# Operand copies on another engine, row sums from the matrix product, and a new order of units in an encoder step

## The reference, cut to what matters

```python
h = rmsnorm(x); u = h @ w_in                  # mixer columns, memory queries, gate
A: softmax(q k^T / 8 + bias) v                # 12 heads of 64, band of 8 chunks of 64 tokens
B: o = (softmax(q1 k1^T/8 - alibi) - lam * softmax(q2 k2^T/8 - alibi)) v   # 6 heads, v of 128
   o = rmsnorm(o)
C: q = rmsnorm(cq) @ w_uq                     # 12 heads of 64 + 32 rotated columns
   k, v = rmsnorm(ckv) @ w_ukv                # latent of 256, values of 64
   softmax((qn kn^T + qr kr^T) * scale) v     # chunk-causal, all earlier keys
M: softmax(mq mk^T / 8) mv
x += (concat(mixer, M) * silu(gate)) @ w_out
```

## Time and profile before

| | |
|---|---|
| median of 3 runs | 3321.17 us (3317.43 to 3321.68) |
| profiled execution: time, span | 3319.59 us, 3317.7 us |
| mean granted clock of PE | 0.91 of full |
| PE busy | 2822.7 us (85%) |
| VectorE busy | 1540.5 us (46%) |
| ScalarE busy | 1216.2 us (37%) |
| GpSimd busy | 834.4 us (25%) |
| chain that ended last | PE 64%, VectorE 17%, ScalarE 10%, issue 4%, GpSimd 4% |

### The profile page before, as it was taken

The page is one execution under the profiler, slowest core; times in us unless marked ns, Lnnn a source line. Parts: engine busy times, 40 slices in busy tenths (PEclk is TensorE's granted clock), DMA queues, the critical chain, the costliest instruction groups (busy, mean ns, idle before and its releaser), DMA issues.

```text
span 3317.7 us, 46359 instructions
## 1 busy us (share of the span) xinstructions
PE 2822.7 (85%) x18786; PEld 2631.0 (79%) x18786; DVE 1540.5 (46%) x3502; ACT 1216.2 (37%) x2680; POOL 834.4 (25%) x434
## 2 busy tenths in 40 slices
PE   4888999978979889879888677777779888999987
PEld 4788999978878878869877566667669788999877
DVE  7205565551135666751222256665651215655542
ACT  3323444432234444442232234434341224444431
POOL 7522222204322122204311222222203312212212
PEclk8999999989989999979997878888879999999989
DMA  3311111113111111113110000000013111111111
GB/s 143 101 49 38 54 51 45 55 63 103 40 39 49 55 58 52 49 62 94 54 39 27 23 13 9 6 9 6 14 49 98 55 39 51 45 47 59 51 66 65
DMA packets 55892, 167.90 MB, mean 51 GB/s; under 512 B 6464, under 2 KB 14272, under 8 KB 55168
## 3 DMA queue, kind: packets, MB, share of 16 engines
q1 hardware_dynamic: 55680, 164.94, 14.7%
HBM read 131.13 MB, written 33.79 MB: 50 GB/s over the span
## 4 chain that ended last, share of the span: by engine, by line
PE 64%; DVE 17%; ACT 10%; issue 4%; POOL 4%; DMA 1%; SPq 0%; DVEq 0%; ACTq 0%
PE acc L1363 30%; PE acc L1342 9%; PE acc L1426 8%; PE scores L1384 8%; PE turned L1396 5%; ACT prob L957 5%; DVE prob L1155 3%; DVE pt_split L1185 3%; PE scores L1295 2%; POOL h_split L1237 2%; DVE raw L1043 2%; ACT pt_split L966 2%; DVE prob L1178 2%; DVE prob L1175 1%; POOL w_lo L1229 1%
## 5 line engine op out<-in xcount | busy, mean ns | idle before, releaser
L1363 PE MATMUL acc<-h_split,w_hi 128*128 128x352 f32 (+3 forms) x5116 | 1263.3, 330 | 84.4 <-POOL w_lo L1229 40.6
L1363 PEld LDWEIGHTS acc<-h_split,w_hi 128*128 128x128 f32 x5116 | 899.6, 194 | 109.0 <-POOL w_lo L1229 44.4
L1229 POOL TENSOR_TENSOR w_lo<-w_raw,w_hi 128x1024 fp32r<-128x1024 f32 (+2 forms) x172 | 390.1, 2271 | 1946.5 <-ACT w_hi L916 1946.5
L1363 PE MATMUL acc<-h_split,w_lo 128*128 128x352 f32 (+3 forms) x2558 | 833.2, 326 | 0.0
L957 ACT ACTIVATE prob<-prob,stat 128x256 f32<-128x256 f32 (+9 forms) x576 | 386.0, 671 | 532.1 <-DVE stat L1155 532.0
L1426 PE MATMUL acc<-pt_split,v_split 128*64 128x256 f32 (+4 forms) x3486 | 487.4, 280 | 73.5 <-DVE pt_split L1185 63.5
L1185 DVE TENSOR_TENSOR pt_split<-turned,pt_split 128x512 fp32r<-128x512 f32 (+4 forms) x564 | 303.0, 552 | 519.3 <-ACT pt_split L966 518.7
L1363 PEld LDWEIGHTS acc<-h_split,w_lo 128*128 128x128 f32 x2558 | 496.2, 194 | 0.0
L1426 PEld LDWEIGHTS acc<-pt_split,v_split 128*64 128x64 f32 (+1 forms) x3486 | 389.2, 156 | 98.5 <-DVE pt_split L1185 81.0
L1396 PE MATMUL turned<-ident,prob 128*128 128x128 f32 (+2 forms) x1866 | 301.4, 287 | 147.4 <-DVE prob L1179 86.2
L1155 DVE CUSTOM_DVE_ANT_0 prob<-scores,bias 128x256 f32<-128x256 f32 (+9 forms) x576 | 338.1, 633 | 186.2 <-PE scores L1384 182.9
(11 more groups left out here) (102 smaller groups left out, 2805.4 us busy)
## 6 DMA issues: line engine op xcount, KB each, us to landing
w_raw<-w SPq DMA_DIRECT2D x148, 512.0 KB, 3.5
x_scr<-y_sb SPq DMA_DIRECT2D x24, 528.0 KB, 5.3
y_sb<-x_scr SPq DMA_DIRECT2D x24, 528.0 KB, 5.7
bias<-rel_in SPq DMA_DIRECT2D x24, 320.0 KB, 4.2
raw<-kcache SPq DMA_DIRECT2D x18, 256.0 KB, 3.8
v_cache<-vcache SPq DMA_DIRECT2D x18, 256.0 KB, 3.7
y_sb<-x_in SPq DMA_DIRECT2D x8, 528.0 KB, 5.9
y_out<-raw SPq DMA_DIRECT2D x8, 528.0 KB, 2.7
```

What stands on the lines that cost most here:

```text
L1229: pool.tensor_tensor(w_lo[:, n % 2, 0:wide], w_raw[:, n % 2, 0:wide], w_hi[:, n % 2, 0:wide].bitcast(F32), ALU.subtract).then_inc(wlo_made ...
L1363: ins = pe.matmul(acc[s.bank][:, 0:s.cols], (w_hi, w_lo)[ws][:, w, 128 * k:128 * k + 128], x(xs, k), start=k == 0 and y == 0, stop=k == s. ...
```

## The change: what it does, and the diff

1. The high halves of queries and keys (`conv`) are copied by ScalarE instead of VectorE. The two parts are cut anew: A, B: first 512 columns; C: half of queries and keys each.
2. In C no probabilities are normalised before the product. Columns of ones stand beside the values' high halves, so that the product with 128 columns gives values in rows 0 to 63 and the sums of the probabilities in rows 64 to 127. ScalarE takes logarithm and exp(-x) of the sums, VectorE multiplies by the gate (`evac`) after the logarithms and by the reciprocals in a new item `emul`. The exponentials write no row sum. The accumulator is free for PE once it was multiplied by the gate.
3. The three passes of pv are in a new order, the outer loop over passes: (value high, p high), (value low, p high), then (value high, p low). PE waits for the chunk's high halves first and for its low halves only before the third pass. All kinds of job.
4. The order of units is 1, 2, 0, 3, 4 for A, B, C, and the side products are spread as (2, 1, 3, 2, 1) for A and B and (3, 3, 5, 3, 1) for C.
5. Buffers: values' halves laid out anew, the probabilities' buffer shorter, some small buffers share places. GpSimd sets the ones once, at the start of layer C.

```diff
+PV_PASSES = ((0, 0), (1, 0), (0, 1))
-PROB = 5632
+PROB = 4928
-    for g in (0, 1, 2, 3) if job.kind == "M" else (0, 2, 1, 3):
+    for g in (0, 1, 2, 3) if job.kind == "M" else (1, 2, 0, 3):
-BESIDE = {"M": (1, 1, 1, 0, 0), "A": (2, 2, 2, 2, 1), "B": (2, 2, 2, 2, 1), "C": (3, 4, 4, 3, 1)}
+BESIDE = {"M": (1, 1, 1, 0, 0), "A": (2, 1, 3, 2, 1), "B": (2, 1, 3, 2, 1), "C": (3, 3, 5, 3, 1)}
                 if narrow:
                     self.scores(nxt, 1)
+                if prev is not None:
+                    order.append(("emul", prev))
-        return (slice(0, 256), slice(0, 256)) if part == 0 else (slice(256, TOK), slice(256, KEYS))
+        return (slice(0, 512), slice(0, 512)) if part == 0 else (slice(512, TOK), slice(512, KEYS))
-            half, quarters = TOK // 2, slice(0, 1) if part == 0 else slice(1, 4)
+            half, quarters = TOK // 2, slice(2 * part, 2 * part + 2)
 ...
 def scalar_program
+                    if u.job.kind != "C":
                         act.activation(p, p, ACT.Exp, scale=-1.0, bias=..., accum_out=...)
+                    else:
+                        act.activation(p, p, ACT.Exp, scale=-1.0, bias=...)
+            elif name == "conv":
+                ... (the waits that VectorE had)
+                for i, (x, hi, _) in enumerate(splits_of(job, part)):
+                    act.activation(hi, x, ACT.Copy).then_inc(operand_hi.mark(job.n, part, i), 1)
+            elif name == "evac" and item[1].job.kind == "C":
+                u = item[1]
+                act.wait_ge(*pv_done.upto(u.chunks[-1].p))
+                if u.before.job.kind == "C":
+                    act.wait_ge(*o_read.upto(u.before.n))
+                for lane in range(2):
+                    act.activation(recip[64 * lane:64 * lane + 64, 0:u.qn], acc[0][64:128, 256 * lane:256 * lane + u.qn],
+                                   ACT.Ln).then_inc(sums_logged.mark(u.n), 1)
+                act.wait_ge(*sums_logged.upto(u.n))
+                act.activation(recip[:, 0:u.qn], recip[:, 0:u.qn], ACT.Exp, scale=-1.0).then_inc(sum_recips.mark(u.n), 1)
 ...
 def vector_program
-            elif name == "conv":
-                ...
-                    dve.tensor_copy(hi, x).then_inc(operand_hi.mark(job.n, part, i), 1)
-            elif name == "N":
+            elif name == "N" and item[1].job.kind != "C":
 ...
+                    if u.job.kind == "C":
+                        dve.wait_ge(*sums_logged.upto(u.n))
                     for lane in range(2):
                         ins = dve.tensor_tensor(gate, acc[0][0:64, ...], gate, ALU.mult)
-                    ins.then_inc(o_read.mark(u.n), 1)
+                    ins.then_inc((o_gated if u.job.kind == "C" else o_read).mark(u.n), 1)
+            elif name == "emul" and item[1].job.kind == "C":
+                dve.wait_ge(*o_gated.upto(u.n))
+                dve.wait_ge(*sum_recips.upto(u.n))
+                dve.tensor_tensor(gate, gate, recip[:, 0:u.qn], ALU.mult).then_inc(o_read.mark(u.n), 1)
 ...
 def pool_program
+                elif what == "operands" and more["kind"] == "C":
+                    pool.wait_ge(*normed_hi.upto(norm_key, KT - 1))
+                    pool.memset(v_hi[:, :, :, 64:128].bitcast(F32), 1.0).then_inc(ones_set.mark("values"), 1)
 ...
 def tensor_program
-                pe.wait_ge(*o_read.upto(held.n))
+                pe.wait_ge(*(o_gated if held.job.kind == "C" else o_read).upto(held.n))
-                if c == 0:
+                if c == 0 and u.job.kind != "C":
                     pe.wait_ge(*probs_ready.upto(u.tiles[-1].n))
+                elif c == 0:
+                    pe.wait_ge(*exps_ready.upto(u.tiles[-1].n, 1))
-                pe.wait_ge(*turned_lo.upto(chunk.a))
+                pe.wait_ge(*turned_hi.upto(chunk.a))
-                for i, (lane, block, n, src, dst, w) in enumerate(chunk.mults):
-                    for y, (vs, ps) in enumerate(PASSES):
+                for y, (vs, ps) in enumerate(PV_PASSES):
+                    if y == 2:
+                        pe.wait_ge(*turned_lo.upto(chunk.a))
+                    for i, (lane, block, n, src, dst, w) in enumerate(chunk.mults):
+                        if job.kind == "B":
+                            rows, values = 128, vb_sp[0:n, vs, block, :]
+                        elif vs == 0 and job.kind == "C":
+                            rows, values = 128, v_hi[0:n, block, lane, :]
+                        elif vs == 0:
+                            rows, values = 64, v_hi[0:n, block, lane, 0:64]
+                        else:
+                            rows, values = 64, v_lo[0:n, block, lane, :]
```

More of the change, by code:

```diff
@@ L350, in stream @@
         self.times_v(last, len(last.chunks) - 1)
-        order.append(("evac", last))
+        order += [("evac", last), ("emul", last)]
         if last.job.kind == "B":
@@ L967, in scalar_program @@
                 ins.then_inc(turned_hi.mark(chunk.a), 1)
+            elif name == "conv":
+                _, job, part = item
+                if part == 0:
+                    if job.before is not None:
+                        act.wait_ge(*scores_ready.upto(job.before.units[-1].tiles[0].n))
+                    if job.kind == "M":
+                        act.wait_ge(*side_read.upto(job.sides["mq"][-1].n))
+                        act.wait_ge(*kcache_loaded.upto(job.n))
+                    elif job.kind == "C":
+                        act.wait_ge(*side_read.upto(job.sides["ck"][-1].n))
+                        act.wait_ge(*rotated.upto(job.n, 1, 2))
+                    else:
+                        act.wait_ge(*side_read.upto(job.sides["k"][-1].n))
+                elif job.kind in "AB":
+                    act.wait_ge(*kcache_loaded.upto(job.n))
+                for i, (x, hi, _) in enumerate(splits_of(job, part)):
+                    act.activation(hi, x, ACT.Copy).then_inc(operand_hi.mark(job.n, part, i), 1)
             elif name == "vt":
@@ L1192, in vector_program @@
                 dve.wait_ge(*turned_hi.upto(a))
[L1193 to L1195 removed]
+                hi, lo = halves_of_v(job.kind, rows, block, n)
+                dve.tensor_tensor(lo, split_v(t_ps[a % 2][0:rows, 0:128 * n]), hi.bitcast(F32),
+                                  ALU.subtract).then_inc(turned_lo.mark(a), 1)
             elif name == "evac":
```

93 lines of the change are left out of this document (47 added, 46 removed).

## The result

The changed kernel takes 3298.67 us (median of 5 runs, 3291.63 to 3304.14) and the kernel before, beside it on the same chip, 3319.28 (5 runs, 3317.43 to 3321.68): ratio 0.9935, 95% interval 0.9920 to 0.9951. It is 20.6 us faster. I had forecast 68 less, so the sign was right, the size a third of what I said, and the time lies inside my range (3150 to 3322), near its upper end, but outside the 3215 to 3290 that I gave the forecast itself. The profiled execution took 3300.31 us with a span of 3298.1 (before 3317.7); the mean granted clock rose from 0.910 to 0.913, and the time at the lower level fell from 600 to 575 us of the span.

The account below looks back on a forecast made before the run. PE is busiest, and in C what it waits for is VectorE's queue, not its load. Terms for A, B, C, memory jobs and ones sum to -68.5 us from 3319.6, giving 3251 (median 3252); range 3150 to 3322.

Parts of the forecast that it names:

- ten A jobs 0: Term for the ten A jobs with another job behind them: no change in their time, 0 us.
- under -5: Term for memory jobs and the start of C: ScalarE's copies take 5.8 us for 9.0, so -5 us.
- The order's step: B jobs: the new order of units removes the 5.6 us wait before unit 3; sum of waits 8.0 to 4.7 us.
- with the 5.6 gone most of the 7 us at half clock: 2.4 us: B jobs: without the long wait most low clock goes too, saving 2.4 us of a job's 5.7.
- 2.6 instead of 4.3: C jobs, unit 3: with copies on ScalarE, two blocks stop PE by 2.6 us in all instead of 4.3.
- -2.2 +1.6: C jobs without normalisation: waits of 3.7 us become 1.5, while wider weights cost PE 1.6 us a job.
- The last C: Term for the last C job, without side products or rotation: waits 19.8 to 12, clock -3, weights +1, together -10 us.
- the two last A: Term for the two last A jobs: shorter waits for low halves from the new passes, -8 us together.
- The last B: Term for the last B job: -2 us, its wait of 7 us staying because unit 0 has nothing beside it.
- Unit 0 of C decides: Rival, chance 0.15: after the 6.6 us wait the clock stays low through units 0, 3 and 4; C +14 a job, 3339 us.
- C opens up: Rival, chance 0.2: the long wait in C doesn't come, the clock stays at 2.4 GHz, C takes 71.3 us; time 3150.
- ScalarE takes VectorE's place: Rival, chance 0.15: ScalarE's queue stops PE as long; C gains 0, B's gain is half eaten; 3305 to 3320 us.

Follow-up runs that it names:

- a_order: The changed kernel with A's old order of units and old side-product counts beside A and the memory jobs before A or B: 3275.01 us, ratio 0.9869.
- rows_last: The changed kernel with the products of the 32-key block after all others, their three passes together: 3277.08 us, ratio 0.9874.
- order_rows: The changed kernel with both the edits of a_order and rows_last: 3263.75 us, ratio 0.9831.
- copies_v: The changed kernel with operand high halves copied by VectorE again before memory, A and B jobs, ScalarE only before C: 3313.12 us, ratio 0.9976.
- c_rot: The changed kernel with the rotation of the odd head's queries issued behind the second wide score tile: 3282.76 us, ratio 0.9876.
- copies_c_v: The changed kernel with only C's operand high halves copied by VectorE again: 3329.00 us, ratio 1.0027.
- norm_c: The changed kernel with C's probabilities normalised by VectorE as before, without sums beside the values: 3314.83 us, ratio 0.9983.

## Why the prediction was wrong

**The step that failed is the term "ten A jobs 0".** Its only ground is "In A and B a block is 1.2 to 1.7 us, and a chunk holds 2 us and more of PE work: nothing, at most 0.5 a job if the cover is gone". So for a full A job I had weighed only the copies. The change also gave A a new order of units, new side counts and new passes, and I weighed the first two for B and C only and the passes for the last A and C. The prediction itself says that nothing can be won in A; it doesn't ask what can be lost. A full A job had 0.7 us idle. It grew by 0.8 us of waits (a_order takes them away), 0.4 us for row switches (rows_last), some 0.3 us more that PE is busy in the new order (65.7 for 65.4 in a_order), and by 1.4 us for a fall of the clock in four of ten: 20.7 us for the ten. In the old order and with the switches mended A is back at 65.7 with the copies still on ScalarE (order_rows), so the copies cost nothing there; in the new order they cost 0.6 (copies_v), a part of the same lost cover. The memory jobs are the same fault: their order did not change, but the counts beside them did, and in layer 0 PE waits 1.8 us for probabilities that the old counts covered. They are 2.1 to 2.4 us longer each; a_order takes that away in layers 0 and 3 and 1.4 of the 2.4 in layer 1. I had them under -5. Together the two kinds are 28 of the 48 us by which I missed.

**B, -16.7 for -28.** The order's step held: no wait of 5.6, 4.2 idle for 4.7 forecast, 2.1 us where I said 2.5. (The working has 7.7 and then 8.2 us for the same stretch of PE's work; ahead of unit 3 no wait was left by either.) The term that failed is "with the 5.6 gone most of the 7 us at half clock: 2.4 us". In one job the low clock did go whole. What it had cost there can be read from the same instructions at both levels. In the kernel before, behind the transposes of the earlier trace rows:

```profile
1173.44 1.62 PE L1384 MATMUL scores<-k_split,q_split 64*32 64x512 f32 x12
1175.00 0.77 PE L1363 MATMUL acc<-h_split,w_hi 128*128 128x352 f32 x2
```

and in the changed kernel, at full clock:

```profile
1177.44 0.60 PE L1447 MATMUL turned<-ident,prob 128*128 128x128 f32 x4
...
1178.60 0.95 PE L1433 MATMUL scores<-k_split,q_split 64*32 64x512 f32 x12
1179.49 0.59 PE L1412 MATMUL acc<-h_split,w_hi 128*128 128x352 f32 x2
```

From the transposes to the side product is 3.77 us at 1.2 GHz and 2.05 at 2.4, and the side product's first pair takes 0.18 more: 1.9 us in all, since 2.6 of the 6.8 us of low clock lay over idle time, which the higher clock does not shorten. PE's busy time fell by only 1.1 (63.1 to 62.1): row switches took 0.4 back, and the rest is other work of the new order. That is a job 5.0 us shorter, for 5.7 forecast. The other four, with the same waits, kept 3.4 to 7.9 us of low clock with PE busy in all of it, and the mean job is 68.2: this is most of what B missed. The copies, which I had at 0 in B, are worth 4.6 a job in the new order (copies_v: 363.9 for five jobs), so the new order with VectorE copying is slower than the kernel before (357.8).

**C, -17.1 for -14 in four jobs, came as worked out, wait by wait.** In unit 0 and ahead of it 1.2 + 6.1 + 1.1 = 8.4 us for 9.0 forecast, and c_rot shows that the rotation holds the longest; behind the even head's rotation 2.6 for 2.2; at the copies in unit 3 2.5 for 2.6; behind the exponentials of the decode unit 1.3 for 1.5; low clock 19 to 24 us for 23. What I had wrong is what the parts are worth. "2.6 instead of 4.3" makes the copies' move 1.7 us a job. It counts the longer of two waits there (the other, at 2099.08 us, was 1.7), and it left out that GpSimd lengthens VectorE's copies, and copies_c_v puts it at 5.6 to 7.2, low clock included. (That kernel copies in the new parts, so a share of it can be theirs.) Normalisation: -2.2 +1.6 a job came to nothing in a job between others, and is worth 5 to 6 us in the first and in the last (norm_c), where I had no term for it by itself. `emul` came at 0.43 us, well under the 0.81 that I took as its nearest row. The last C fell short by 3.2 us and the two last A by 2.5 together: part of both is low clock that came or went with position, and I can't say how much.

**The last B** stayed at 55.8: 1.7 us less idle time met 6.5 us more low clock. In ten of the twelve kernels above it takes 50.7 to 53.3 with 18 to 20.5 us idle.

**The rivals.** "Unit 0 of C decides" did not happen: after 6.1 us of idle time the clock was low for 6.8 us, not for 43. "C opens up" did not happen either, since the rotation stands where I said. "ScalarE takes VectorE's place" is refuted for B and C by both kernels that give the copies back.

**The tells.** B near 65.5: 66.2 to 69.4. C near 89: 87.4 to 88.7, with one wait of 5 to 7 us and its named releaser. VectorE near 43 us of a C job: 42.0. A still 65.8: 66.7 to 68.7, which the text had named as a sign of failure, though for another reason (the copies). The products of C at 0.11 us can't be read in the changed kernel, since its decode units lie in low clock; in rows_last one stands at full clock (from 2011.56 us) and its 30 products take 3.06 us, 0.10 each and 1.0 more than the 2.05 of the earlier trace rows, for 1.2 forecast.

What stays open: what fixes where the clock falls. The runs show that the same work, with no idle time, is followed by a fall in one place and by none in another, and that edits in one layer move falls in others. That part of a change's gain (in B up to 3 us a job) I could not have read from the trace of before. Nor did a run separate, in A, the order of units from the counts of side products, or the new parts of the copies from their move.

## What to carry to other kernels

When an edit touches a table or an order that several stages share, write a term for every stage that reads it, the ones at their bound first: a stage with 1% idle time has next to nothing to win from an order and can lose. Low clock that lies over idle time returns nothing when the wait goes; price the rest by the same instructions at the higher clock, and keep a case in which the clock stays low without the wait. Before moving copies off an engine, look at what each copy of the same size costs alone and beside the other engine's work: the price that goes away is the second.

## What the runs showed of the hardware

- Narrow products (32 columns on weights of 64) begin 0.06 us apart; where the number of rows changes between 128 and 32, the next begins 0.13 to 0.14 us later and the one behind it 0.08. Five such switches for one made a group of 30 take 2.45 us for 2.05.
- VectorE's copy of 96x528 took 0.42 us with GpSimd idle and 1.54 behind one of its subtractions; 64x784 took 0.55 where it began first and 2.19 behind one (copies_c_v). On ScalarE they took 0.63 and 0.85 beside the same subtractions, which themselves ran in 1.31 and 1.86 us for 1.6 and 2.0.
- The clock fell to 1.2 GHz for 3.4 us behind a stretch in which PE was never idle (30 narrow products and four transposes), and did not fall behind the same stretch elsewhere. In B, jobs of equal waits (4.1 us idle) took 66.2 us with no low clock and 69.4 with 7.9.
